# A causal depthwise convolution on TensorE: one 158-column matmul per channel in place of a 128- and a 30-column one, stored with its overlap

## The reference

```python
proj = h @ w_in          # q, forget, input, output gate | glu value, glu gate | merge gates A, B
# mixer A: HGRN2 recurrence, 8 heads with 128x128 states, chunks of 64 frames
# mixer B:
u = glu_v * sigmoid(glu_g)                       # (S, 1024)
u = causal_depthwise_conv(u, conv_w, conv_b)     # 31 taps: frame t sees t-30..t, each channel alone
u = silu(layer_norm(u, conv_ln_g, conv_ln_b))
y_b = u @ w_conv_out
# merge, output projection, residual + LayerNorm, SwiGLU (2816 hidden), residual + LayerNorm
```

## Time and profile before

| | |
|---|---|
| median of 3 runs | 2410.17 us |
| profiled execution, slowest core (6) | 2407.3 us |
| TensorE (PE) busy | 2281.7 us, 95% |
| DVE / ACT / POOL busy | 1251.1 / 965.1 / 438.5 us |
| DMA | 423 MB, 176 GB/s on average |
| median of die 0 / die 1 | 2397.8 / 2401.5 us |

### The profile page before, as it was taken

The page is one execution under the profiler, slowest core; times in us unless marked ns, Lnnn a source line. Parts: engine busy times, 40 slices in busy tenths (PEclk is TensorE's granted clock), DMA queues, the critical chain, the costliest instruction groups (busy, mean ns, idle before and its releaser), DMA issues.

```text
span 2407.3 us, 39689 instructions; the slowest of 8 cores (2389.8 to 2407.3 us)
## 1 busy us (share of the span) xinstructions
PE 2281.7 (95%) x14037; PEld 1133.9 (47%) x14288; DVE 1251.1 (52%) x1830; ACT 965.1 (40%) x1262; POOL 438.5 (18%) x547
## 2 busy tenths in 40 slices
PE   5999989999998988899999999999999999999997
PEld 2555545555554543344444444444444444444443
DVE  1777757676776775733533533623623623621514
ACT  4766756665566763341231232222223223211210
POOL 0111111011101332211311411411411310300210
PEclk9999999999999999999999999999999999999999
DMA  8676997888757778654654664664674574464451
GB/s 230 92 100 120 146 159 134 130 146 159 152 155 191 185 264 252 218 185 152 229 200 166 201 216 160 210 228 153 201 234 169 183 244 142 168 213 152 153 173 66
DMA packets 117363, 423.01 MB, mean 176 GB/s; under 512 B 9760, under 2 KB 42656, under 8 KB 87968
## 3 DMA queue, kind: packets, MB, share of 16 engines
q1 hardware_dynamic: 101296, 368.70, 47.7%
q0 software_dynamic: 15872, 51.74, 15.7%
HBM read 430.20 MB, written 70.58 MB: 208 GB/s over the span
## 4 chain that ended last, share of the span: by engine, by line
PE 84%; DMA 5%; DVE 4%; issue 3%; ACT 3%; POOL 0%; SPq 0%; DVEq 0%; ACTq 0%; POOLq 0%
PE pst L447 83%; DMA ys<-sb_y_19_61 2%; DMA sb_stg_20_62<-xt 1%; PE pst L459 1%; DMA sb_stg_20_62<-w 1%; DVE sb_R_70_112 L492 1%; ACT L474 1%; DVE sb_u_15_57 L492 1%; DVE sb_R_50_92 L492 0%; ACT sb_F_26_68 L474 0%; DMA sb_W_12_54<-w2b 0%; ACT sb_rs_43_85 L474 0%; DVE sb_Qp_71 L492 0%; DVE sb_u_14_56 L492 0%; ACT sb_osq_78 L474 0%
## 5 line engine op out<-in xcount | busy, mean ns | idle before, releaser
L447 PE MATMUL pst<-sb_W_12_54,sb_xT_55 128*128 128x512 bf16 (+1 forms) x742 | 151.4, 352 | 28.1 <-ACT sb_xT_55 L573 25.0
L474 ACT ACT_TABLE_LOAD x121 | 155.2, 1283 | 24.8 <-DVE sb_q_76_118 L483 12.8
L447 PE MATMUL pst<-sb_xT_55,sb_W_8_50 128*128 128x512 bf16 x550 | 128.5, 384 | 11.8 <-DVE sb_v_75 L500 4.5
L447 PE MATMUL pst<-sb_W_9_51,sb_xT_55 128*128 128x256 bf16 (+1 forms) x756 | 120.4, 308 | 4.6 <-ACT sb_og_32_74 L474 1.9
L447 PE MATMUL pst<-sb_xT_55,sb_W_10_52 128*128 128x512 bf16 x512 | 119.7, 383 | 4.1 <-ACT sb_y_19_61 L504 1.7
L447 PEld LDWEIGHTS pst<-sb_W_12_54,sb_xT_55 128*128 128x128 bf16 x768 | 75.0, 100 | 89.0 <-issue 34.0
L447 PE MATMUL pst<-sb_hT_93,sb_W_12_54 128*128 128x512 bf16 x501 | 113.0, 379 | 2.0 <-ACT sb_hT_93 L504 1.4
L447 PE MATMUL pst<-sb_hT_93,sb_W_10_52 128*128 128x512 bf16 x502 | 112.6, 379 | 0.5
L447 PE MATMUL pst<-sb_hT_93,sb_W_72_114 128*128 128x512 bf16 x499 | 112.4, 379 | 0.7
L447 PE MATMUL pst<-sb_hT_93,sb_W_8_50 128*128 128x512 bf16 x468 | 107.7, 385 | 2.4 <-ACT sb_hT_93 L504 1.9
L951 POOL TENSOR_TENSOR sb_st_78_120<-sb_st_78_120,sb_cst_43 128x1 f32<-128x1 f32 x16 | 8.9, 554 | 549.8 <-DVE sb_st_78_120 L488 549.8
(11 more groups left out here) (317 smaller groups left out, 4525.8 us busy)
## 6 DMA issues: line engine op xcount, KB each, us to landing
sb_W_8_50<-w2b SPq DMA_DIRECT2D x36, 1024.0 KB, 6.4
sb_W_12_54<-w2b SPq DMA_DIRECT2D x36, 1024.0 KB, 6.2
sb_W_9_51<-w2b SPq DMA_DIRECT2D x36, 1024.0 KB, 6.6
sb_W_10_52<-w2b SPq DMA_DIRECT2D x34, 1024.0 KB, 6.0
sb_W_71_113<-w2b SPq DMA_DIRECT2D x34, 1024.0 KB, 6.3
sb_W_72_114<-w2b SPq DMA_DIRECT2D x32, 1024.0 KB, 6.4
w2b<-w POOLq DMA_DIRECT2D x54, 512.0 KB, 10.7
sb_T_16_58<-tabb SPq DMA_DIRECT2D x32, 632.0 KB, 7.3
```

The costliest lines, as they stand in the source:

```text
L447: i = e.matmul(o, lhsT=l, rhs=r, start=s0, stop=s1)
L474: P.add("act", lambda e: e.activation(out=out, in_=in_, func=func, **kw), ks(in_, scale, bias) + list(er), (ks(out) if wkeys is None else ...
```

## The change

- A conv unit becomes two halves of 8 channels. A half is 8 matmuls of 158 columns, two groups of four, in its own "c" bank (316 of 512 columns). Nothing is accumulated over blocks: the 30 sums for the next block are stored beside the 128.
- There are three store buffers [128 x 316], one to a half in turn. A half's store is 162 KB, in runs of 1264 B, into `ys`, now [unit, (4 channels x 32 blocks), 2 x 158]. The channels are permuted to suit (`pack_taps`).
- In phase 2 the 128 own sums of a block come by `load_cpre` with 16 DMAs (runs of 512 B), the 30 sums from the block before by `load_tails` with 16 more (runs of 120 B) into the tiles `tls`, and `conv_ln` adds them with two DVE additions of 128 x 16 x 30 before anything else.
- The planner's cost of a half is 0.16 us (0.65 for a whole unit before), a store's bytes 220000 (600000).

```diff
-        yst = [A.at(f"y{i}", yo + i * 2048, [128, 4, 128], F32) for i in range(2)]
+        yst = [A.at(f"y{i}", yo + i * 1280, [128, 2, TW], F32) for i in range(3)]
...
+        tls = [A.at(f"tl{i}", uo + 24576 + i * 2048, [128, 4, 4, NTL], F32) for i in range(2)]
+        tls += [inU("tl2", [128, 4, 4, NTL], F32), inR("tl3", [128, 4, 4, NTL], F32)]
...
+        def dmas(eng, pairs, whole, sem, rd=(), nbytes=0):
+            if sem not in dsems:
+                dsems[sem] = es.enter_context(nc.semaphore("d_" + sem))
+            P.add(eng, lambda e: [e.dma_start(out=o, in_=i) for o, i in pairs], list(rd), ks(whole), dsem=sem,
+                  dur=0.1 * len(pairs), lat=2.0, nb=nbytes, nd=len(pairs))
...
         def conv_unit(q, g):
-            ps = newps("c")
-            for gr in range(4):
-                for tail in range(2):
-                    for j in range(4):
-                        o = ps[32 * j:32 * j + NBLK, gr * 128:gr * 128 + (30 if tail else 128)]
-                        lh = u[:, cl, (1 if tail else 2):(1 if tail else 2) + NBLK]
-                        rh = T[:, ti + 128:ti + 158] if tail else T[:, ti:ti + 128]
-                        lst.append((o, lh, rh, not tail, bool(tail)))
-            P.ops[-1]["dur"] = 0.65
-                cp_any(ys[r0:r0 + n, :, ::-1], ps[r0:r0 + n].rearrange("p (a b) -> p a b", a=4), scale=0.5)
-                dma("sp", dst, ys[r0:r0 + n], f"y{G % 2}_{jj}", wr=[("ys", G, jj)], nbytes=600000)
-            relps("c", ps)
+            for hf in range(2):
+                g8 = 2 * g + hf
+                U_ = q * 32 + g8
+                ps = newps("c")
+                c0 = [g8 // 16 * 128 + gr * 64 + g8 % 16 * 4 for gr in range(2)]
+                mmg([(ps[32 * j:32 * j + NBLK, gr * TW:(gr + 1) * TW], u[:, c0[gr] + j, 2:2 + NBLK],
+                      T[:, (hf * 8 + gr * 4 + j) * TW:(hf * 8 + gr * 4 + j + 1) * TW], True, True)
+                     for gr in range(2) for j in range(4)], ...
+                P.ops[-1]["dur"] = 0.16
+                ys = yst[U_ % 3]
+                cp_any(ys[:, :, ::-1], ps[:, 0:2 * TW].rearrange("p (a b) -> p a b", a=2), scale=0.5)
+                dma("sp", ys_d[U_ * 128:(U_ + 1) * 128, :], ys[:].rearrange("p a b -> p (a b)"), f"y{U_ % 3}_0",
+                    wr=[("ys", U_)], nbytes=220000)
+                relps("c", ps)
             if g + 2 < CG:
                 conv_load(q, g + 2)
...
-        def load_cpre(i, qs=range(4)):
+        def load_cpre(i, qs=range(4), tails=True):
             for q in qs:
-                src = bass.AP(ys_h, 2 * q * 128 * S + i * TS, [[S, 128], [128 * S, 2], [1, TS]])
-                dma("sp", cpre[:, 2 * q:2 * q + 2, :], src, f"cp{q}", ..., nbytes=440000)
+                prs = [(cpre[gr * 64:gr * 64 + 64, ch, :].rearrange("p (b t) -> p b t", b=4),
+                        bass.AP(ys_h, ch * 64 * CS + 4 * i * RS + gr * TW + NTL, [[CS, 64], [RS, 4], [1, 128]]))
+                       for gr in range(2) for ch in (2 * q, 2 * q + 1)]
+                dmas("sp", prs, cpre[:, 2 * q:2 * q + 2, :], f"cp{q}", ..., nbytes=600000)
+            if 3 in qs and tails:
+                load_tails(i)
+
+        def load_tails(i):
+            b0 = 1 if i == 0 else 0
+            for hf in range(2):
+                tl = tls[(i > 0) * 2 + hf]
+                if b0:
+                    memset(tl[:, :, 0, :], 0.0)
+                prs = [(tl[gr * 64:gr * 64 + 64, ch % 4, b0:4, :],
+                        bass.AP(ys_h, ch * 64 * CS + (4 * i + b0 - 1) * RS + gr * TW, [[CS, 64], [RS, 4 - b0], [1, NTL]]))
+                       for gr in range(2) for ch in range(4 * hf, 4 * hf + 4)]
+                dmas("sp", prs, tl[:], f"{'ct' if i else 'cu'}{hf}", ..., nbytes=250000)
...
         def conv_ln(i):
+            for hf in range(2):
+                o = cpre[:, 4 * hf:4 * hf + 4, :].rearrange("p c (b t) -> p (c b) t", b=4)[:, :, 128 - NTL:128]
+                tt_(o, o, tls[(i > 0) * 2 + hf][:].rearrange("p c b t -> p (c b) t"), ALU.add)
```

More of the change, by code:

```diff
@@ L40 @@
 TAB_N = 128 * 1266
+NUC = D // 8
+NTL = TW - 128
 class Prog:
@@ L55, in __init__, with add @@
         self.bias = 0
-    def add(self, eng, fn, reads=(), writes=(), dsem=None, dur=0.3, lat=0.0, tbl=None, prio=0, nb=0, alts=None):
+    def add(self, eng, fn, reads=(), writes=(), dsem=None, dur=0.3, lat=0.0, tbl=None, prio=0, nb=0, alts=None, nd=1):
         i = len(self.ops)
@@ L223, in body @@
                     if op["dsem"] is not None:
-                        inst.then_inc(dsems[op["dsem"]], 16)
+                        for one in inst if isinstance(inst, list) else [inst]:
+                            one.then_inc(dsems[op["dsem"]], 16)
                     elif op["sig"]:
@@ L654, in conv_unit @@
-            mmg(lst, rk=ks(T[:], u[:, g * CG:(g + 1) * CG, :]) + [("u", q % 2, "z")] +
-                [("u", q % 2, b) for b in range(NBLK)])
-            P.ops[-1]["dur"] = 0.65
[L657 to L662, removed]
-                cp_any(ys[r0:r0 + n, :, ::-1], ps[r0:r0 + n].rearrange("p (a b) -> p a b", a=4), scale=0.5)
-            for jj, (r0, n) in enumerate(rows):
-                dst = bass.AP(ys_h, (G * CG + jj) * S, [[128, n], [4 * S, 4], [1, 128]])
-                dma("sp", dst, ys[r0:r0 + n], f"y{G % 2}_{jj}", wr=[("ys", G, jj)], nbytes=600000)
@@ L667, in conv_unit @@
-            relps("c", ps)
+            for hf in range(2):
[5 more added lines that the diff above has]
+                      T[:, (hf * 8 + gr * 4 + j) * TW:(hf * 8 + gr * 4 + j + 1) * TW], True, True)
+                     for gr in range(2) for j in range(4)],
+                    rk=ks(T[:, hf * 8 * TW:(hf + 1) * 8 * TW], u[:, c0[0]:c0[0] + 4, :], u[:, c0[1]:c0[1] + 4, :]) +
+                    [("u", q % 2, "z")] + [("u", q % 2, b) for b in range(NBLK)])
+                P.ops[-1]["dur"] = 0.16
[4 more added lines that the diff above has]
+                relps("c", ps)
@@ L874, in loads @@
             dma("sp", (on2 if i else on0)[:], ons_d[i], "on2", rd=[("ons", i, p) for p in range(4)], nbytes=750000)
-        def load_cpre(i, qs=range(4)):
+        RS = 2 * TW
+        CS = NBLK * RS
+        def load_cpre(i, qs=range(4), tails=True):
             for q in qs:
-                src = bass.AP(ys_h, 2 * q * 128 * S + i * TS, [[S, 128], [128 * S, 2], [1, TS]])
-                dma("sp", cpre[:, 2 * q:2 * q + 2, :], src, f"cp{q}",
-                    rd=[("ys", G, jj) for G in range(q * CG, (q + 1) * CG) for jj in range(4)], nbytes=440000)
+                prs = [(cpre[gr * 64:gr * 64 + 64, ch, :].rearrange("p (b t) -> p b t", b=4),
+                        bass.AP(ys_h, ch * 64 * CS + 4 * i * RS + gr * TW + NTL, [[CS, 64], [RS, 4], [1, 128]]))
+                       for gr in range(2) for ch in (2 * q, 2 * q + 1)]
+                dmas("sp", prs, cpre[:, 2 * q:2 * q + 2, :], f"cp{q}",
+                     rd=[("ys", U_) for U_ in range(32 * q, 32 * q + 32)], nbytes=600000)
+            if 3 in qs and tails:
[9 more added lines that the diff above has]
+                       for gr in range(2) for ch in range(4 * hf, 4 * hf + 4)]
+                dmas("sp", prs, tl[:], f"{'ct' if i else 'cu'}{hf}", rd=[("ys", U_) for U_ in range(NUC)], nbytes=250000)
         def load_R(i):
@@ L1039, in tail_b @@
             yield from conv_ln(0)
-            load_cpre(1)
+            load_cpre(1, tails=False)
             yield
@@ L1086, in build_nc @@
         P.epoch = 8
+        load_tails(1)
         load_R(0)
@@ L1196, in pack_taps @@
     base = np.arange(D) * TW + 127
+    n = np.arange(D)
+    order = n // 128 * 128 + n // 4 % 2 * 64 + n // 8 % 16 * 4 + n % 4
     for d in range(TAPS):
-        tab[base + d] = conv_w[TAPS - 1 - d]
+        tab[base + d] = conv_w[TAPS - 1 - d][order]
     return tab.reshape(128, TAB_N // 128)
```

10 lines of the change are left out of this document (3 added, 7 removed).

## The result

The changed kernel is slower: the ratio to the kernel before is 1.0382, 95% interval 1.0351 to 1.0413, that is about 2502 us against 2409.87 (+92). The median of its six runs reads 2614.03 because some of them fell into a state in which one die runs slower; the ratio leaves these out. The profiled execution spans 2504.0 us, 97 more than the one before.

What follows compares the result with a forecast made beforehand. TensorE, 95% busy, was taken to bound the kernel, with phase 2 almost full and holes in phase 1. Terms 5 + 3 + 8 + 23 + 3 + 3 + 10 = +55 on 2407.3, plus 3, gave 2465 us, range 2412 to 2530.

Steps and rivals of the forecast that it cites:

- rival C: Phase 2: a tail tile of small pieces takes 10 to 23 us, total 2497 to 2555; chance 0.15.
- the forecast: Whole kernel: the main case with all terms summed, 2465 us, own range 2445 to 2500; chance 0.45.
- Matmuls and visits: Conv on TensorE: merged matmuls give −4, 31 more visits by 0.3 cost +9; net +5 us.
- evacuations: Conv evacuations on ACT and DVE: 39 us become 57, mostly hidden; +3 us (0 to 10).
- Store buffers: Phase 1: three half buffers reused sooner make evacuations wait for stores; +8 us (−12 to +30).
- The burst: Conv's end: its last 12 halves back to back, TensorE waiting for stores and tables; +23 us (10 to 33).
- the clock: TensorE's clock falling with the wait at the conv's last 12 halves; +3 us.
- End of phase 1: Conv ends earlier, easing some waits, but block 0's LayerNorm needs 16 + 16 DMA issues; +3 us (−12 to +12).
- Phase 2: Additions on DVE wait for later loads, delaying ffn1 products and TensorE in 6 blocks; +10 us (0 to 60).
- Rival B: Phase 1: store round trips get short, ending stalls and easing the end; 2400, 2385 to 2410 us; chance 0.08.
- the entry: TensorE's switch into a conv unit: 1.39 us after six 512-column steps began, called 0.09 too much.
- the chances: Whole kernel's outcome: within 2% 0.51, slower 0.46, faster by over 2% 0.03.

Runs made afterwards that it cites:

- e_split: The change with four buffers and rows 1280 B apart, each channel again in two matmuls of 128 and 30 columns; ratio 1.0179 to the kernel before.
- e_b4: The kernel before with only the conv units halved, four half buffers, aligned 512 B runs, no tails; ratio 1.0083 to the kernel before, +20 us.
- e_pad: The change with the conv result's rows in HBM 1280 B apart instead of 1264; ratio 1.0168 to the kernel before, +41 us.
- e_b4_odd: e_b4 with everything in ys 48 B further in HBM; ratio 1.0395 to the kernel before, +95 us.
- e_b3: The kernel before with only the conv units halved, three half buffers, aligned 512 B runs, no tails; ratio 1.0158 to the kernel before, +38 us.
- e_join: The change with two halves going out by one 316 KB store from two buffers of 16 channels, rows unpadded; ratio 1.0216 to the kernel before, +52 us.
- e_four: The change with four store buffers for halves in place of three; ratio 1.0234 to the kernel before, +56 us.
- e_dur65: The change with the planner booking 0.65 us for a half instead of 0.16; ratio 1.0278 to the kernel before, +67 us.
- e_four_pad: The change with four store buffers and rows 1280 B apart together; ratio 1.0158 to the kernel before, +38 us.
- e_full: The change with four buffers and rows of 1280 B written whole instead of 1264 B of them; ratio 1.0162 to the kernel before.

## Why the prediction was right in direction and short in size

The time of 2502 lies in the range (2412 to 2530), 37 us over the point, on the side of "slower". Part of that is luck. The range went up to 2530 because of phase 2 and rival C, and nothing was lost in phase 2; 2502 is 2 us over the forecast's own 2445 to 2500 and fits rival C's 2497 to 2555 by the number alone. By place, steps 6 to 24 lost 60 us where the terms made 16 (matmuls, evacuations, buffers), and the rest lost 36.6 where they made 39, with a phase 2 of 10 in it that didn't come. By its steps:

- **Matmuls and visits, +5; evacuations, +3.** The merging is worth what it was priced at: 4 us, where e_split's rows make 5 to 6. Of the visits and evacuations, e_b4 shows the price: with 91 visits and 128 evacuations but neither merging nor tails it is +20, where the two terms without the merging made 12, with bounds of 3 and 23. It holds the halves' stores as well, so the two aren't parted.
- **Store buffers, +8.** This is the step that failed, by size and by mechanism. I asked when a buffer is used again and how late a store lands, took the landing from the rows of before, and let the longer runs speak for shorter landings ("a store is 162 KB in runs of 1264 B rather than 256 KB in 512 B"). I didn't ask where those runs start. Rows of 1264 B put three of four starts off a multiple of 64 B; before, every run started at a multiple of 512. (Which multiple matters isn't shown: padded rows start at multiples of 256.) The median landings rose from 7.3 to 10.6 for the tables, and steps 6 to 24 lost 60 us. e_pad gives 36 of these back, e_b4_odd makes a loss of 48 in the same stretch of e_b4 with nothing else changed, and e_b3 shows that the reuse distance, which I had priced, costs some 5 us by itself. It matters where landings are late: the fourth buffer is worth 32 us with unpadded rows and 7 with padded. e_join, which gets 40 us back with rows at odd starts, says that this isn't the whole mechanism.
- **The burst, +23 and +3 for the clock.** Right in mechanism, and in the wait itself: the period I gave, 1.3 to 2.7 us a half, was 2.3, and TensorE waits 22.4 us in it. It stands at 868 to 896 us, not around 700 to 800 as I had written. But this wait isn't what the run of halves costs. The versions without a run pay most of it elsewhere: from step 24 on they are faster by 8 us (e_four), 3 (e_dur65), and 6 with padded rows (e_four_pad against e_pad). Padding gives 12 there.
- **End of phase 1, +3.** Steps 28 to 30 are +3.3 and the rest to the end −16.0. This is not the waits that I thought the change would ease (the lower bound of −12), for the idle time from step 30 on is the same: the work stands earlier now.
- **Phase 2, +10.** Nothing came, and here the path was wrong. I had priced eight issues at 3.0 us; they took 7.0 and 5.1 (one takes 601 ns at the median, not 371). But the additions of phase 2 didn't wait for them (two at the passage did, 8.9 us in all). On SP each tile's loads stand right behind the addition that frees the tile, so they are for the next block, some 180 us ahead of their use. What the additions waited for is the load of the 128 own sums (23.3 us in ten waits of at most 4.7), and TensorE lost nothing by it. DVE in `ffn1` of a block, then SP, then the wait and the first and last start of the loads and the additions:

```profile
1365.85 0.66 DVE L488 TENSOR_TENSOR sb_cpre<-sb_cpre,sb_tl 128x480 f32<-128x480 f32 x1 [1.21 <-DMA sb_cpre<-ys]
...
1374.26 0.66 DVE L488 TENSOR_TENSOR sb_cpre<-sb_cpre,sb_tl 128x480 f32<-128x480 f32 x1 [2.78 <-DMA sb_cpre<-ys]
```

```profile
1366.97 7.01 SPq L539 DMA_DIRECT2D sb_tl<-ys  x8
1374.13 0.48 SPq L533 DMA_DIRECT2D sb_W<-w2b  x1
1375.04 5.08 SPq L539 DMA_DIRECT2D sb_tl<-ys  x8
```

```profile
DVE sb_cpre L488 <- DMA sb_cpre<-ys: 23.3, 10, 4.7
...
L539 SPq DMA_DIRECT2D sb_tl<-ys x128: 573/601/2152, 904.4 to 1751.5; - x128
L488 DVE TENSOR_TENSOR sb_cpre<-sb_cpre,sb_tl x16: 651/658/660, 912.9 to 1931.9; 128x480 f32<-128x480 f32 x16
```

- **Rival C**, dear pieces of 120 B, is out. The tails' DMAs landed in 4.1 us at the median, each with 256 pieces of 120 B:

```profile
sb_tl<-ys SPq DMA_DIRECT2D x112, 30.0 KB, 4.1
```

The Trainium skill's 512 B for line rate (DMA: Bandwidth & Descriptors, Specifications) thus did not decide anything here: small reads were cheap, and what was dear were larger writes at odd starts. **Rival B** needed short round trips and got longer ones.

- **Slips of the sum.** The six steps before a unit make 6 by 0.22 = 1.32 us, so the entry is 0.07 too long and not 0.09, and the chances add up to 0.52 within 2% and 0.45 slower, not 0.51 and 0.46. Neither changes the forecast.

What stays open: e_four_pad is 18 us over e_b4, 12.5 of them in steps 6 to 24. e_split and e_full exclude the matmuls and the rows' ends as the cause; the evacuation of 316 columns for 256, a quarter more bytes, and another order remain, and I have not parted them. Why writes at odd starts hold up other transfers is not shown, only that they do. And why joining two stores takes most of that away without moving a row (e_join) is not shown either; a joined store with padded rows, which would tell whether the two gains are one, was not run.

## What to carry to other kernels

When a change gives an array in HBM a new row length, look at where the rows start before you count buffers: here padding 1264 B to 1280 was worth 51 us of 92, and the sign was a later landing of transfers that the change hadn't touched. Read the planner's order for runs of one kind of work: twelve halves without cover, each of which needs a table and a buffer from memory, ran at the memory's pace. But price such a run by the whole rest of the program, since a stretch that gets longer may hold more work. Before you price a wait that an order seems to show, ask for which block the transfer is. And ask what a merged instruction can give at most: 0.12 us a unit here, 5 to 6 us in all, against which every new transfer, store and visit has to stand.
